# Where the buffers of a two-block transformer kernel lie in SBUF: activations of the second block in their own tile, weight buffers at several offsets

## What is computed

```
def first_block(x, ...):
    h = concat([meta, x])                        # 272 x 2048
    proj = rmsnorm(h, mix_norm_g) @ w_in         # q, k, v, cq, ckv, k_pe
    out_a = neighbourhood_attention(q_a, k_a, v_a, ...)
    out_b = mla_attention(cq, ckv, k_pe, ...)
    h = h + concat([rmsnorm(out_a), rmsnorm(out_b)]) @ w_out
    g, u = rmsnorm(h) @ w_gate, rmsnorm(h) @ w_up           # 2048 -> 5632
    h = h + (silu(conv(g)) * u) @ w_down
    return h[:, 16:]                                        # 256 positions

def second_block(x, c, ...):
    mod = silu(c) @ w_ada + b_ada                           # shifts, scales, gates
    h = rmsnorm(x) * (1 + sc_m) + sh_m
    a_b, a_c, a_x, q, f, i, g, gate_a, gate_b = split(h @ w_in_2)   # 11264 columns
    y_a = (a_b * conv(a_c * a_x)) @ w_conv_out
    y_b = (rmsnorm(hgrn(q, f, i)) * silu(g)) @ w_hgrn_out
    x = x + gt_m * ((sigmoid(gate_a) * y_a + sigmoid(gate_b) * y_b) @ w_o)
    h2 = rmsnorm(x) * (1 + sc_f) + sh_f
    x = x + gt_f * ((silu(h2 @ w_gate_2) * (h2 @ w_up_2)) @ w_down_2)
    return rmsnorm(x)
```

## Time and profile before

| | before |
|---|---|
| median of 3 runs | 2726.02 us |
| the profiled execution: span | 2721.9 us |
| outside the span, against the median | 4.1 us |
| TensorE busy | 2667.9 us (98%), 22052 matmuls |
| TensorE weight loads | 2628.4 us (97%) |
| VectorE / ScalarE / GpSimd busy | 68% / 46% / 12% |
| granted TensorE clock, mean | 0.993 |

### The profile page before, as it was taken

How to read it: one execution, slowest core, us unless ns; L and a number is a source line. 1 busy time by engine, 2 the same in 40 slices (tenths; PEclk the granted TensorE clock), 3 DMA queues, 4 the chain that set the end, 5 groups by cost and what they waited for, 6 DMA issues and landing times.

```text
span 2721.9 us, 51384 instructions
## 1 busy us (share of the span) xinstructions
PE 2667.9 (98%) x22052; PEld 2628.4 (97%) x22052; DVE 1844.2 (68%) x2592; ACT 1250.7 (46%) x1943; POOL 331.3 (12%) x526
## 2 busy tenths in 40 slices
PE   7999999999999999999999999999999999999998
PEld 7888889999999999999999999999999999999998
DVE  6656568877777777787887667766787544444444
ACT  5556655544434444445434443334554443344443
POOL 2110101111111111221000001111211000000001
PEclk9999999999999999999999999999999999999999
DMA  6443345688788888886444578886768656555553
GB/s 202 136 120 91 116 147 178 196 272 272 264 283 273 272 267 274 273 278 205 146 150 154 186 230 275 270 276 212 255 205 270 218 179 193 189 190 190 184 180 122
DMA packets 500084, 571.22 MB, mean 210 GB/s; under 512 B 26704, under 2 KB 473424, under 8 KB 499856
## 3 DMA queue, kind: packets, MB, share of 16 engines
q1 hardware_dynamic: 467968, 463.76, 52.2%
q0 software_dynamic: 31600, 103.80, 11.7%
q10 hardware_dynamic: 288, 0.36, 0.0%
HBM read 565.77 MB, written 2.54 MB: 209 GB/s over the span
## 4 chain that ended last, share of the span: by engine, by line
PE 88%; DVE 7%; ACT 3%; issue 1%; DMA 0%; POOL 0%; SPq 0%; DVEq 0%; ACTq 0%
PE ps L691 27%; PE ps L692 27%; PE ps L693 26%; DVE wl L1798 3%; ACT wh L1288 1%; PE ps L989 1%; PE ps L820 1%; PE ps L658 1%; PE ps L660 1%; PE ps L659 1%; DVE nx L1902 1%; DVE lr L1994 1%; DMA raw<-in_w_in 0%; PE ps L836 0%; PE ps L846 0%
## 5 line engine op out<-in xcount | busy, mean ns | idle before, releaser
L1798 DVE TENSOR_TENSOR wl<-raw,wh 128x1024 fp32r<-128x1024 f32 (+1 forms) x894 | 1059.2, 1201 | 594.6 <-ACT wh L1288 590.0
L691 PE MATMUL ps<-xx,wh 128*128 128x256 f32 (+3 forms) x4720 | 1343.6, 285 | 9.3 <-DVE xx L1879 5.2
L692 PE MATMUL ps<-xx,wh 128*128 128x256 f32 (+3 forms) x4720 | 1325.3, 281 | 0.0
L693 PE MATMUL ps<-xx,wl 128*128 128x256 f32 (+3 forms) x4720 | 1322.4, 280 | 0.0
L1288 ACT ACTIVATE wh<-raw 128x1024 fp32r<-128x1024 f32 (+1 forms) x894 | 883.8, 1030 | 618.6 <-PE ps L693 600.1
L691 PEld LDWEIGHTS ps<-xx,wh 128*128 128x128 f32 (+1 forms) x4720 | 889.3, 188 | 16.5 <-DVE wl L1798 9.7
L692 PEld LDWEIGHTS ps<-xx,wh 128*128 128x128 f32 (+1 forms) x4720 | 889.6, 188 | 1.7 <-issue 1.0
L693 PEld LDWEIGHTS ps<-xx,wl 128*128 128x128 f32 (+1 forms) x4720 | 889.4, 188 | 0.0
L692 PE MATMUL ps<-hid,wh 128*128 128x256 f32 x1408 | 393.8, 280 | 0.0
L691 PE MATMUL ps<-hid,wh 128*128 128x256 f32 x1408 | 393.8, 280 | 0.0
L693 PE MATMUL ps<-hid,wl 128*128 128x256 f32 x1408 | 392.8, 279 | 0.0
(11 more groups left out here) (370 smaller groups left out, 2521.3 us busy)
## 6 DMA issues: line engine op xcount, KB each, us to landing
raw<-in_w_in SPq DMA_DIRECT2D x118, 1024.0 KB, 5.3
ada_raw<-in_w_ada POOLq DMA_DIRECT2D x384, 256.0 KB, 4.8
raw<-in_w_gate SPq DMA_DIRECT2D x44, 1024.0 KB, 6.5
raw<-in_w_up SPq DMA_DIRECT2D x44, 1024.0 KB, 6.9
raw<-in_w_ffn_gate SPq DMA_DIRECT2D x44, 1024.0 KB, 5.3
raw<-in_w_ffn_up SPq DMA_DIRECT2D x44, 1024.0 KB, 5.6
raw<-in_w_down SPq DMA_DIRECT2D x32, 1024.0 KB, 6.3
raw<-in_w_ffn_down SPq DMA_DIRECT2D x32, 1024.0 KB, 5.4
```

The lines of the kernel that those rows point to most:

```text
L691: pe.matmul(dst, h[:, c, o:o + w], x[:, 0, k, g.t0:g.t1], start=(k == 0), stop=False)
L692: pe.matmul(dst, h[:, c, o:o + w], x[:, 1, k, g.t0:g.t1], start=False, stop=False)
L693: m = pe.matmul(dst, l[:, c, o:o + w], x[:, 0, k, g.t0:g.t1], start=False, stop=end)
L1798: dve.tensor_tensor(wl[i % NS][:, part], raw[i % NR][:, part], wh[i % NS][:, part].bitcast(F32), ALU.subtract).then_inc(s_lo, 1)
```

## The change

It changes where tiles lie, and nothing else. The instructions of every engine, their shapes and their waits follow each other as before; only the operand `xx` is `xs` in the second block.

- `xs`, [2, 17, 256], lies over `xx` and is the second block's activations. Every chunk is 1024 bytes and starts at 64 modulo 256 (`row_home(xoff, 64)`); the 17th chunk is never used and only spaces the halves. `ffn` takes the operands of gate and up as arguments, `norm_dst` and the splits of `merged` write to `xs`. Activations read by `gemm_raw` in the second block (`raw_mix`, part of `xx`, `raw_ffn`) keep their tiles.
- Five buffers of 1088 bytes (`rstd`, three `ssq`, one `sqt`) are put between the six weight buffers, so `wh0`, `wh1`, `wh2` start at 128, 192, 0 and `wl0`, `wl1`, `wl2` at 64, 128, 192. `xx` then starts at 192.
- `hid` starts at 128, `conv` at 0, `oo` stays at 192; `raw_ffn` and `raw_mix` move with `hid`, from 192 to 128.

```diff
@@ -96,9 +97,8 @@
 NXB = 3
-NSQ = 2
 NGC = 3
-X0, XQ, XKV, XB, XHID, XOC, XOH = "x", "q", "kv", "b", "hid", "oc", "oh"
+X0, XS, XQ, XKV, XB, XHID, XOC, XOH = "x", "s", "q", "kv", "b", "hid", "oc", "oh"
 PAIR = [(0, 128), (128, 128)]
@@ -153,31 +153,31 @@
-    def ffn(b, wg, wu, wd, t0):
+    def ffn(b, wg, wu, wd, gate_x, up_x):
         for f in range(2):
             for g in range(HALF // 2):
-                add((b, "gate", f, g), wg, 0, 16, 128 * (HALF * f + 2 * g), 256, X0, t0, T, PAIR, [0, 1])
-                add((b, "up", f, g), wu, 0, 16, 128 * (HALF * f + 2 * g), 256, X0, 16, T, PAIR, [2, 3])
+                add((b, "gate", f, g), wg, 0, 16, 128 * (HALF * f + 2 * g), 256, *gate_x, PAIR, [0, 1])
+                add((b, "up", f, g), wu, 0, 16, 128 * (HALF * f + 2 * g), 256, *up_x, PAIR, [2, 3])
             for g in range(8):
...
-    ffn(1, "w_gate", "w_up", "w_down", 14)
+    ffn(1, "w_gate", "w_up", "w_down", (X0, Q0, T), (X0, META, T))
     for p in range(4):
         for n, c0 in (("q", 3072), ("f", 4096), ("i", 5120), ("g", 6144)):
-            add((n, p), "w_in_2", 0, 16, c0 + 256 * p, 256, X0, 16, T)
+            add((n, p), "w_in_2", 0, 16, c0 + 256 * p, 256, XS, 0, SEQ)
     for p in range(4):
         for n, c0 in (("ac", 1024), ("ax", 2048), ("ab", 0)):
-            add((n, p), "w_in_2", 0, 16, c0 + 256 * p, 256, X0, 16, T)
+            add((n, p), "w_in_2", 0, 16, c0 + 256 * p, 256, XS, 0, SEQ)
     for gs in [(g,) for g in range(6)] + [(6, 7)]:
         for g in gs:
-            add(("ga", g), "w_in_2", 0, 16, 7168 + 256 * g, 256, X0, 16, T)
-            add(("gb", g), "w_in_2", 0, 16, 9216 + 256 * g, 256, X0, 16, T)
+            add(("ga", g), "w_in_2", 0, 16, 7168 + 256 * g, 256, XS, 0, SEQ)
+            add(("gb", g), "w_in_2", 0, 16, 9216 + 256 * g, 256, XS, 0, SEQ)
         for g in gs:
...
     for g in range(8):
-        add(("wo", g), "w_o_2", 0, 16, 256 * g, 256, X0, 16, T)
-    ffn(2, "w_ffn_gate_2", "w_ffn_up_2", "w_ffn_down_2", 16)
+        add(("wo", g), "w_o_2", 0, 16, 256 * g, 256, XS, 0, SEQ)
+    ffn(2, "w_ffn_gate_2", "w_ffn_up_2", "w_ffn_down_2", (XS, 0, SEQ), (XS, 0, SEQ))
     return slabs, gemms, order
@@ -320,13 +320,28 @@
+        def row_home(offset, place):
+            return offset + (place - offset) % ROW_BYTES
+
         def sem(name):
...
         raw = [sb(f"raw{i}", [P, SLAB]) for i in range(NR)]
-        wh = [sb(f"wh{i}", [P, SLAB], F32R) for i in range(NS)]
-        wl = [sb(f"wl{i}", [P, SLAB], F32R) for i in range(NS)]
+        ssq, wh, wl = {}, [], []
+        wh.append(sb("wh0", [P, SLAB], F32R))
+        rstd = sb("rstd", [P, T])
+        wh.append(sb("wh1", [P, SLAB], F32R))
+        ssq["h"] = sb("ssq_h", [P, T])
+        wh.append(sb("wh2", [P, SLAB], F32R))
+        ssq["a"] = sb("ssq_a", [P, T])
+        wl.append(sb("wl0", [P, SLAB], F32R))
+        ssq["b"] = sb("ssq_b", [P, T])
+        wl.append(sb("wl1", [P, SLAB], F32R))
+        sqt = [sb("sqt0", [P, T])]
+        wl.append(sb("wl2", [P, SLAB], F32R))
+        xoff = cursor[0]
         xx = sb("xx", [P, 2, KD, T], F32R)
+        xs, _ = at("xs", [P, 2, KD + 1, SEQ], F32R, row_home(xoff, 64))
         hoff = cursor[0]
@@ -337,13 +352,11 @@
         nx = [sb(f"nx{i}", [P, T]) for i in range(NXB)]
-        sqt = [sb(f"sqt{i}", [P, T]) for i in range(NSQ)]
+        sqt.append(sb("sqt1", [P, T]))
         ada_off = cursor[0]
...
         mod = sb("mod", [P, 96])
-        rstd = sb("rstd", [P, T])
-        ssq = {n: sb(f"ssq_{n}", [P, T]) for n in "hab"}
         arena = cursor[0]
@@ -382,24 +395,26 @@
         raw_in, _ = at("raw_in", [P, 2, KD, T], F32R, limit // 32 * 32 - 8 * KD * T)
-        raw_ffn = [at(f"raw_ffn{i}", [P, 2, 8, T], F32R, arena + (2 + 22 * i) * SEQ * 4)[0] for i in range(2)]
-        raw_mix, _ = at("raw_mix", [P, 2, 6, T - Q0], F32R, arena + 2 * HALF * SEQ * 4)
-        cursor[0] = arena
+        ffn_home = row_home(arena, 128)
+        raw_ffn = [at(f"raw_ffn{i}", [P, 2, 8, T], F32R, ffn_home + (2 + 22 * i) * SEQ * 4)[0] for i in range(2)]
+        raw_mix, _ = at("raw_mix", [P, 2, 6, T - Q0], F32R, ffn_home + 2 * HALF * SEQ * 4)
+        cursor[0] = ffn_home
         hid = sb("hid", [P, 2, HALF, SEQ], F32R)
...
-        cursor[0] = arena
+        cursor[0] = mix_home = row_home(arena, 0)
         conv = sb("conv", [P, 2, 8, SEQ], F32R)
+        cursor[0] = oo_home = row_home(cursor[0], 192)
         oo = sb("oo", [P, 2, 8, SEQ], F32R)
...
         hsets = [None, {n: sb(f"hg1_{n}", [P, 2, SEQ]) for n in "qfkig"}]
-        keep, cursor[0] = cursor[0], arena
+        keep, cursor[0] = cursor[0], mix_home
         hsets[0] = {n: sb(f"hg0_{n}", [P, 2, SEQ]) for n in "qfkig"}
...
         hR = sb("hR", [P, 2, SEQ])
-        masks32, _ = at("masks32", [P, nmask], F32, arena + 16 * SEQ * 4)
+        masks32, _ = at("masks32", [P, nmask], F32, oo_home)
         hQs = [sb(f"hQ{i}", [P, 2, SEQ]) for i in range(2)]
@@ -410,8 +425,8 @@
-        OPERAND = {X0: xx, XQ: cqx, XKV: ckvx, XB: xb, XHID: hid, XOC: conv, XOH: oo}
-        NORM_DST = [xx, cqx, ckvx, xb, xx, xx, xx, xx]
+        OPERAND = {X0: xx, XS: xs, XQ: cqx, XKV: ckvx, XB: xb, XHID: hid, XOC: conv, XOH: oo}
+        NORM_DST = [xx, cqx, ckvx, xb, xx, xx]
         NORM_T0 = [0, Q0, 0, Q0, Q0, Q0, 16, 16]
@@ -443,6 +458,9 @@
             return H[:, i, NORM_T0[n]:T]
+
+        def norm_dst(n, h, i):
+            return NORM_DST[n][:, h, i, NORM_T0[n]:T] if n < N_MIX2 else xs[:, h, i, :]
@@ -1078,8 +1096,8 @@
                         pool.wait_ge(s_nh, NORM_X[n] + i + 1)
-                    pool.tensor_tensor(NORM_DST[n][:, 1, i, t0:T], bufs[i % len(bufs)][:, 0:m],
-                                       NORM_DST[n][:, 0, i, t0:T].bitcast(F32), ALU.subtract).then_inc(s_nlp, 1)
+                    pool.tensor_tensor(norm_dst(n, 1, i), bufs[i % len(bufs)][:, 0:m],
+                                       norm_dst(n, 0, i).bitcast(F32), ALU.subtract).then_inc(s_nlp, 1)
                     yield from paced(n, i)
@@ -1387,7 +1405,7 @@
                     x = nx_bufs(n)[i % len(nx_bufs(n))][:, 0:m]
-                    h = NORM_DST[n][:, 0, i, t0:T]
+                    h = norm_dst(n, 0, i)
                     act.wait_ge(s_nx, NORM_X[n] + i + 1)
@@ -1743,7 +1761,7 @@
                     act.wait_ge(s_mg, c + 1)
-                    act.activation(xx[:, 0, c, 16:T], merged[:, c, :], ACT.Copy).then_inc(s_mgh, 1)
+                    act.activation(xs[:, 0, c, :], merged[:, c, :], ACT.Copy).then_inc(s_mgh, 1)
@@ -2412,7 +2430,7 @@
                 dve.wait_ge(s_mgh, c + 1)
-                dve.tensor_tensor(xx[:, 1, c, 16:T], merged[:, c, :], xx[:, 0, c, 16:T].bitcast(F32), ALU.subtract).then_inc(s_mgl, 1)
+                dve.tensor_tensor(xs[:, 1, c, :], merged[:, c, :], xs[:, 0, c, :].bitcast(F32), ALU.subtract).then_inc(s_mgl, 1)
```

More of the change, by code:

```diff
@@ L28 @@
 SLAB = 2048
+ROW_BYTES = 256
 ORDER = "q0 m0 k0 v0 q1 m1 k1 v1 m2 q2 k2 v2 m3 q3 k3 v3".split()
@@ L1431, in finish @@
                 for i in range(8):
-                    act.activation(NORM_DST[n][:, 0, i, Q0:T], norm_src(n, i), ACT.Copy, scale=norm_gain(n, i)).then_inc(s_ah, 1)
+                    act.activation(norm_dst(n, 0, i), norm_src(n, i), ACT.Copy, scale=norm_gain(n, i)).then_inc(s_ah, 1)
                     if i % 4 == 3:
@@ L1875, in low @@
                     x = nx_bufs(n)[i % len(nx_bufs(n))][:, 0:m]
-                    h, l = NORM_DST[n][:, 0, i, t0:T], NORM_DST[n][:, 1, i, t0:T]
+                    h, l = norm_dst(n, 0, i), norm_dst(n, 1, i)
                     dve.wait_ge(s_nh, NORM_X[n] + i + 1)
@@ L1927, in finish @@
                 for i in range(8):
-                    h = NORM_DST[n][:, 0, i, Q0:T]
+                    h = norm_dst(n, 0, i)
                     dve.wait_ge(s_ah, heads_base(n) + i + 1)
-                    dve.scalar_tensor_tensor(out=NORM_DST[n][:, 1, i, Q0:T], in0=norm_src(n, i), scalar=norm_gain(n, i), in1=h.bitcast(F32),
+                    dve.scalar_tensor_tensor(out=norm_dst(n, 1, i), in0=norm_src(n, i), scalar=norm_gain(n, i), in1=h.bitcast(F32),
                                              op0=ALU.mult, op1=ALU.subtract).then_inc(s_al, 1)
```

## The result

The changed kernel takes 2728.15 us (median of 20 runs, 2722.57 to 2730.39), the kernel before 2722.76 us (20 runs, 2717.45 to 2726.29). The ratio is 1.0016, 95% interval 1.0010 to 1.0023: 0.16% slower, 4.4 us, inside the 0.2% that I called no change, and clear of zero. I had forecast 2719 us, faster. The sum started from the median of three runs, 2726.02 us, which lies 3.3 us above that of twenty; from 2722.76 the same working gives 2715.5. No instruction was added or moved; what could move is the distance between matmuls, and it did, in both directions.

The account below looks back on a forecast made before the run. TensorE's distance between matmul starts was taken as the bound. Quick pairs' 14.2 us against 6.9 us already saved gave -7.3, the rest 0: span 2721.9 to 2714.6, plus 4.1 to the median, 2719 us; range 2693 to 2739.

Parts of the forecast that it names:

- What bounds the kernel: Whole kernel: TensorE, busy 98%, sets the time as number of matmuls times distance between starts; other engines' address changes cost 0.
- What the place acts on: Gemm matmuls: the distance from moving operand to weights loaded meanwhile, modulo 256, sets the pace, not the place alone.
- the place alone: Rival, `xs` and `hid`: place 64 is quick whatever the weights do, `xs` saves 31 us; 2697 us, chance 0.20.
- The price: `xs` and `hid`: a matmul at distance 192 costs 113.3 ns at best, any other 117.7, 4.4 ns apart.
- Three quarters, from the only row that has it: `xs` and `hid`: quick pairs pay three quarters of 18.9 us, 14.2 us, as `xx` did; net -7.3 us.
- The rest at nothing, bounds of 2.8 us: `conv`, `oo` and first block's matmuls on 258, 272 and `up`'s 256 columns: 0 us; first block bounded 2.8 us either side.
- the second term: The zero for the rest, beside the -7.3 us from quick pairs; first block's bounds 2.8 us either side.
- Pairs never settle: Rival, `xs` and `hid`: changing pairs give 118.0 ns on both, 10.8 us more, 2737 us; decides at 117 ns; chance 0.23.
- Nothing to be measured: Rival: any mix of four distances averages alike (first reason), or only recorded starts are affected; 2726 us, chance 0.17.

Follow-up runs that it names:

- the map: `wh` at 128, `wl` at 128, 192, 0 by slab, `xs` and `hid` at their own place in each block, giving twelve pairs of distances; one run, 2721.71 us.

## Why the prediction was wrong

- *What bounds the kernel* was right: the time moved with the distance between matmul starts, and the splits of VectorE and ScalarE take what they took (1200 ns against 1201, and 1030 in both). What it left out is TensorE's clock after a wait, which moves single executions by some us, as shown above.
- *What the place acts on* was right in its main part. The same pair of distances gives the same value at different places (117.6 to 118.0 for (192,0) and (128,192) on `xs` and `hid`), so it is the distance to the weights that counts, and the rival of the place alone, 2697 us, falls: `xs` at 64 with weights at (128, 64) runs at 117.9. That distances repeat every 256 bytes was assumed throughout and not tested.
- *The price* is the step that failed. "A matmul at distance 192 costs 113.3 ns at best, any other 117.7" treats the distances of `wh` and `wl` as two tolls that add up, by matmul. They don't. 192 to `wh` with 0 to `wl` is worth nothing, (64,128), where I had counted nothing, is worth 1.5 ns, and a pair can have two lasting states, 4.5 ns apart. Of the 14.2 us that I wanted from quick pairs, `xs` gave 59 slabs of 48 matmuls at 116.3 in place of 117.8, 4.2 us, and `hid` none (117.81 ns over 96 slabs, 117.77 before).
- *Three quarters, from the only row that has it*: that row was the price of a way through four places, and I used it for single matmuls whose neighbours are at other distances. The row can't tell a toll of a distance from what a change of distance does.
- *The rest at nothing, bounds of 2.8 us*: the zero was the second term mis-sized, by 2.4 us, and the bounds held. The first block's gate/up stages took 513.4 us against 509.6, but 1.3 of these 3.8 us are the clock: behind the wait at the start of the first stage 38 distances between starts are at the low clock's pace, where it was 25. Sorted by that, the first stage takes 257.7 to 257.8 us with all weights at 128 and 258.6 to 258.7 with weights elsewhere where the low clock was short, and 259.0 to 259.1 against 259.9 to 260.0 where it was long: 0.9 us for the places. The second stage takes 251.9 to 252.0 in the six executions with all weights at 128 and 253.4 in the five with weights elsewhere: 1.5 us. Nearly all of it is `up` on 256 columns, 118.2 ns in place of 116.9; `gate` on 258 goes from 119.6 to 119.7.
- By the traces the places cost +2.4 us in the first block, and in the second `xs` 8640 x (117.37 - 116.96) = +3.5 and `oo` 384 x 1.5 = -0.6. Together 5.3 us, against the measured 4.4 (2.7 to 6.3 by the interval). The second block as a whole differs by only +1.3 in the two traces; 1.0 of the missing 1.6 are ten distances fewer at the low clock's pace in its feed-forward part, the rest is not accounted for.
- *Pairs never settle* had the right sign and the right side of its point, above 117 ns in the gate/up stages, but not its size (118.0 on both; it was 117.4 and 117.8). *Nothing to be measured* is nearest in time, and its first reason is nearly what `xs` did: slabs of the third kind gained 0.7 ns against before, the others lost 0.9 to 1.0.

What stays open: what the two states are, and which feature of an interruption picks one. No row of a trace shows the memory itself. A kernel that enters each pair on purpose from either state was not tried. The splits of ScalarE and VectorE are ruled out above; that TensorE's own weight load is the partner is argued from its overlap with each matmul, and no run shows it by itself.

## What to carry to other kernels

When a kernel is a chain of equal matmuls, its time is the distance between their starts; read that from the count in a window of 100 us, and from one slab on the timeline, since the recorded length says nothing. Where moving and stationary buffers lie to each other is worth a measurement of its own: here 192 modulo 256 to both parts of the weights, in every stage, gave 1.5%, spread weight buffers cost 0.3%, and another fixed pair, (64,192), cost 0.4%. A price read inside a mixed sequence belongs to the sequence; measure the steady case, and more than once. Before two traces are compared by stage, count the matmuls that ran at the lower clock in each.

## What the runs showed of the hardware

- Same program, same window, same granted clock 1.00: 117.8 or 113.3 ns from matmul to matmul. With one pair throughout, the pace changes only after other matmuls or a wait of TensorE; in the map it also changes with the pair of the slab ahead.
- Moving and weight addresses that differ by 0, 64, 128 or 192 bytes modulo 256 put the starts 113.3 to 120.0 ns apart for 256 columns. The Trainium skill ("SBUF — State Buffer", section "Who interferes with whom") has TensorE wait for nobody and its two read ports independent; the rule leaves no room for this spread, and here the measurement decides.
- At a granted clock of 0.50 the starts lie 213 ns apart, in `xs` at (192,192) and in `xx` of the changed kernel alike: no price of a pair is to be seen at the lower clock.
- One execution of 6 of the kernel with spread weights took 10073 us, at a mean granted clock of 0.538. The clock doesn't account for all of it: in its first 3300 us it is recorded as 1.00, but only 137 to 167 matmuls run in 110 us. VectorE's split took 1197 ns there, as ever.
